# Scan decays of two mixers: differences of cumulative log sums, spread by DMA and clipped on GpSimd, instead of TensorE products with masks

## The reference

```python
def segsum(a):
    cs = jnp.cumsum(a, axis=-1)
    diff = cs[..., :, None] - cs[..., None, :]
    mask = jnp.tril(jnp.ones((l, l), dtype=bool))
    return jnp.where(mask, diff, -jnp.inf)

decay = jnp.exp(segsum(adt))                                  # per chunk and head, 128 x 128
y_diag = jnp.einsum('bcgjls,bcsgjp->bclgjp', cb[:, :, :, None] * decay, xg)
```

## Time and profile before

| | us |
|---|---|
| runs of the kernel, median of 3 | 1102.46 (1102.23 to 1104.29) |
| span of the profiled execution, first to last instruction | 1102.2 |
| TensorE busy | 1065.5 (97%) |
| VectorE busy | 662.8 (60%) |
| ScalarE busy | 442.9 (40%) |
| GpSimd busy | 215.7 (20%) |
| DMA, mean rate over the span | 112 GB/s |

### The profile page before, as it was taken

How to read it: one execution, slowest core, us unless ns; L and a number is a source line. 1 busy time by engine, 2 the same in 40 slices (tenths; PEclk the granted TensorE clock), 3 DMA queues, 4 the chain that set the end, 5 groups by cost and what they waited for, 6 DMA issues and landing times. The chain is left out here.

```text
span 1102.2 us, 14509 instructions
## 1 busy us (share of the span) xinstructions
PE 1065.5 (97%) x5590; PEld 876.1 (79%) x5590; DVE 662.8 (60%) x1139; ACT 442.9 (40%) x826; POOL 215.7 (20%) x161
## 2 busy tenths in 40 slices
PE   9999999999989999999899999999999988989997
PEld 5888888888778877788778788887888866878886
DVE  4246435741056687766736866666595667966635
ACT  4223224332256562231623334348624448225432
POOL 0000000000000052201300100002104754135792
PEclk9999999999989999999999999999999999999999
DMA  8276634322042050232324345435212231203501
GB/s 301 81 271 215 215 102 145 114 80 95 11 136 56 10 197 5 73 134 77 125 77 153 115 153 191 153 115 172 91 63 77 63 111 58 77 20 103 185 1 77
DMA packets 58306, 123.89 MB, mean 112 GB/s; under 512 B 5760, under 2 KB 6016, under 8 KB 58112
## 3 DMA queue, kind: packets, MB, share of 16 engines
q1 hardware_dynamic: 55792, 110.22, 29.9%
q0 software_dynamic: 2304, 12.58, 3.2%
q10 hardware_dynamic: 144, 0.20, 0.0%
HBM read 108.83 MB, written 14.16 MB: 112 GB/s over the span
## 5 line engine op out<-in xcount | busy, mean ns | idle before, releaser
L287 DVE TENSOR_TENSOR w_lo<-raw,w_hi 128x2048 fp32r<-128x2048 f32 x58 | 134.3, 2315 | 207.9 <-ACT w_hi L283 196.9
L283 ACT ACTIVATE w_hi<-raw 128x2048 fp32r<-128x2048 f32 x51 | 97.6, 1913 | 211.4 <-PE projections_ps L131 138.3
L129 PE MATMUL projections_ps<-projections_x_hi,w_hi 128*128 128x512 f32 x208 | 81.1, 390 | 0.4 <-ACTq L506 0.4
L130 PE MATMUL projections_ps<-projections_x_lo,w_hi 128*128 128x512 f32 x208 | 80.9, 389 | 0.0
L131 PE MATMUL projections_ps<-projections_x_hi,w_lo 128*128 128x512 f32 x208 | 80.9, 389 | 0.0
L129 PE MATMUL projections_ps<-w_hi,projections_x_hi 128*128 128x512 f32 x192 | 74.7, 389 | 0.0
L130 PE MATMUL projections_ps<-w_lo,projections_x_hi 128*128 128x512 f32 x192 | 74.7, 389 | 0.0
L131 PE MATMUL projections_ps<-w_hi,projections_x_lo 128*128 128x512 f32 x192 | 74.7, 389 | 0.0
L244 DVE SCALAR_TENSOR_TENSOR resid<-resid,mixer_cw 128x512 f32<-128x512 f32 x96 | 64.9, 745 | 0.0
L2480 POOL TENSOR_TENSOR mixer_es<-masks,mixer_gsel 128x1024 f32<-128x1024 f32 x8 | 17.3, 2165 | 229.5 <-PE mixer_ps L1902 152.2
L129 PE MATMUL output_ps<-w_hi,output_m_hi 128*128 128x512 f32 x128 | 52.9, 413 | 2.5 <-DVE output_m_lo L1267 1.4
(11 more groups left out here) (330 smaller groups left out, 2583.3 us busy)
## 6 DMA issues: line engine op xcount, KB each, us to landing
raw<-in_w_in SPq DMA_DIRECT2D x26, 1024.0 KB, 5.0
raw<-in_gdn_w_in SPq DMA_DIRECT2D x24, 1024.0 KB, 5.0
tok<-in_ada_w POOLq DMA_DIRECT2D x16, 768.0 KB, 6.3
raw<-in_w_out SPq DMA_DIRECT2D x8, 1024.0 KB, 5.0
qkv_kept<-mixer_ring SPq DMA_DIRECT2D x8, 1024.0 KB, 4.2
mixer_st<-qkv_kept SPq DMA_DIRECT2D x32, 256.0 KB, 2.9
raw<-in_gdn_w_out SPq DMA_DIRECT2D x8, 1024.0 KB, 5.1
resid<-in_att_bias SPq DMA_DIRECT2D x16, 256.0 KB, 2.7
```

What stands on the lines that cost most here:

```text
L129: nc.tensor.matmul(out, w_hi, x_hi, start=first, stop=False, skip_group_check=True)
L130: nc.tensor.matmul(out, w_hi, x_lo, start=False, stop=False, skip_group_check=True)
L283: self.nc.scalar.activation(self.hi[s][:], self.raw[s][:], ACT.Copy).then_inc(self.hi_ready, 1)
L287: engine.tensor_tensor(self.lo[s][:], self.raw[s][:], self.hi[s][:], ALU.subtract)\
```

## The change

The cumulative sums of the log decays are now made once per mixer, by two small products: one transposed (heads and chunks on the partitions, `logs_t`), one straight (positions on the partitions, `logs`). `logs_t` is written to device memory. For each step or pair, SP loads its eight rows of 128 values, 4 KB, spread to all 128 partitions, 512 KB in all, into `steps_in` or `steps`. GpSimd subtracts the position's own sum and takes the minimum with 0, one instruction for each head and chunk, in place. ScalarE takes the exponential from SBUF instead of PSUM. The products L1015 and L1902 go, and with them TensorE's waits for steps and exponentials. In the scan, the sums are made at the start of attention; in the mixer, ahead of conv block 4. In the mixer the semaphores of the stages before are cleared by GpSimd.

```diff
@@ attention, TensorE and ScalarE
+            nc.tensor.matmul(ps_o[0:LOGS, 1, 0:P], flat_adt, masks[:, UPPER, :], start=True, stop=True)
+            nc.tensor.matmul(ps_o[:, 1, P:P + LOGS], masks[:, UPPER, :], flat_adt, start=True, stop=True).then_inc(logs_made, 1)
...
+                    nc.scalar.activation(logs_t[0:LOGS, :], ps_o[0:LOGS, 1, 0:P], ACT.Copy).then_inc(logs_out, 1)
@@ scan_and_output, SP
+            def load_logs(s):
+                g = s % G
+                if s >= G:
+                    sp.wait_ge(e_ok, s - 1)
+                sp.dma_start(steps_in[:, g].rearrange("p h l -> p (h l)"), a["logs"][s].partition_broadcast(P))\
+                    .then_inc(logs_in[g], 16)
+
+            sp.wait_ge(logs_kept, 16)
+            for s in range(G):
+                load_logs(s)
             sp.dma_start(resid[:], a["x"].rearrange("(t p) d -> p t d", p=P)).then_inc(rows_in, 16)
...
-            for u in range(2, 6):
+            for u in range(2, 4):
                 load_unit(u)
+            for s in range(G, STEPS - 1):
+                load_logs(s)
+            for u in range(4, 6):
+                load_unit(u)
+            load_logs(STEPS - 1)
@@ TensorE, ahead_of
-                pe.wait_ge(steps_ok, s + 1)
-                if s:
-                    pe.wait_ge(e_ok, s)
-                for n in range(2):
-                    mm = nc.tensor.matmul(ps[:, SEG + n, :], below, steps_in[:, g, 4 * n:4 * n + 4, :].rearrange("p a b -> p (a b)"),
-                                          start=True, stop=True)
-                mm.then_inc(seg_made, 1)
@@ ScalarE
-                act.wait_ge(seg_made, s + 1)
+                act.wait_ge(steps_ok, s + 1)
...
-                nc.scalar.activation(E[:, g], ps_seg, ACT.Exp).then_inc(e_ok, 1)
+                nc.scalar.activation(E[:, g], steps_in[:, g], ACT.Exp).then_inc(e_ok, 1)
@@ GpSimd
-                nc.gpsimd.tensor_tensor(steps_in[:, g], upper.unsqueeze(1).broadcast_to([P, HPG, P]),
-                                        adt[:, c, heads_of(g)].unsqueeze(2).broadcast_to([P, HPG, P]), ALU.mult)\
-                    .then_inc(steps_ok, 1)
+                pool.wait_ge(logs_in[g], 16 * (s // G + 1))
+                for n in range(HPG):
+                    h = g * HPG + n
+                    ins = nc.gpsimd.tensor_scalar(steps_in[:, g, n, :], steps_in[:, g, n, :], logs[:, c, h:h + 1], 0.0,
+                                                  ALU.subtract, ALU.min)
+                ins.then_inc(steps_ok, 1)
@@ second_mixer, SP
+            def load_logs(i, j):
+                if j:
+                    sp.wait_ge(e_ok, at(i, 1, j - 1, 1))
+                elif i:
+                    sp.wait_ge(z_ok, 8 * (HB - 1))
+                else:
+                    sp.wait_ge(logs_kept, 16 * TT)
+                sp.dma_start(flat(steps), a["logs2"][i * HB + j].partition_broadcast(P)).then_inc(logs_in, 16)
...
             stage(0, 2)
+            load_logs(0, 1)
             load(B_CONV + 2)
             sp.wait_ge(kk_made, at(0, 1, 1, 1))
             stage(0, 3)
+            load_logs(0, 2)
             sp.wait_ge(kk_made, at(0, 1, 2, 1))
             stage(0, 0)
+            load_logs(0, 3)
...
             stage(1, 2)
+            load_logs(1, 1)
             sp.wait_ge(kk_made, at(1, 1, 1, 1))
             stage(1, 3)
+            load_logs(1, 2)
             sp.wait_ge(kk_made, at(1, 1, 2, 1))
             stage(1, 0)
+            load_logs(1, 3)
@@ TensorE, build
-                pe.wait_ge(steps_ok, at(i, 1, j, 1))
-                if j:
-                    pe.wait_ge(e_ok, at(i, 1, j - 1, 1))
-                if i and j == HB - 1:
-                    pe.wait_ge(m_lo_ok, 8)
-                for n in range(2):
-                    mm = nc.tensor.matmul(psZ[:, n, :], below, flat(steps[:, 4 * n:4 * n + 4, :]), start=True, stop=True)
-                mm.then_inc(seg_made, 1)
@@ ScalarE, exps
-                act.wait_ge(seg_made, at(i, 1, j, 1))
+                act.wait_ge(steps_ok, at(i, 1, j, 1))
...
-                nc.scalar.activation(E, psZ[:].rearrange("p n (m c) -> p (n m) c", c=P), ACT.Exp).then_inc(e_ok, 1)
+                nc.scalar.activation(E, steps, ACT.Exp).then_inc(e_ok, 1)
@@ GpSimd, log_decay_steps
-                nc.gpsimd.tensor_tensor(steps, upper.unsqueeze(1).broadcast_to([P, 8, P]),
-                                        gs.unsqueeze(2).broadcast_to([P, 8, P]), ALU.mult).then_inc(steps_ok, 1)
+                pool.wait_ge(logs_in, 16 * (at(i, 1, j, 1)))
+                for m in range(2 * TT):
+                    h, c = 2 * (i * HB + j) + m // TT, m % TT
+                    ins = nc.gpsimd.tensor_scalar(steps[:, m, :], steps[:, m, :], logs[:, c, h:h + 1], 0.0,
+                                                  ALU.subtract, ALU.min)
+                ins.then_inc(steps_ok, 1)
```

More of the change, by code:

```diff
@@ L298, in channels @@
             for e in range(4):
+                if s == 0 and e == 3 and before_last:
+                    before_last()
                 for kk in range(HALF):
@@ L665, in _, with attention @@
                     w.tokens(pe, i * 2 + (N_Z + j), (N_Z + j) % 2, ps, x_hi, x_lo, banks_free)
-def attention(nc, a, ahead, mix_in, raw, m_g, resid, masks, qk, vals, tok, bias_in):
+def attention(nc, a, ahead, mix_in, raw, m_g, resid, masks, qk, vals, tok, bias_in, adt, logs, logs_t, logs_kept):
     ctx = Phase(nc, "attention")
@@ L868, in _, with scan_and_output @@
                     exponentials(a_next, TILES[3:])
-def scan_and_output(nc, a, ahead, wba, wba_in, mix_in, split, raw, att_f, m_g, masks, small, resid, row_f, tok, xbc, dt, adt, modc,
-                    g_col, gain):
+def scan_and_output(nc, a, ahead, wba, wba_in, mix_in, split, raw, att_f, m_g, masks, small, resid, row_f, tok, xbc, dt, adt, logs,
+                    logs_kept, modc, g_col, gain):
     w_v = a["w_out"][0].rearrange("(k p) c -> p k c", p=P)
@@ L1433, in second_mixer @@
     NB, HB = 2, 4
+    ended = Phase.take_used()
     ctx = Phase(nc, "mixer2")
@@ L1688, in _ @@
                 if n == 6:
+                    sp.wait_ge(logs_out, 2)
+                    rows_out = a["logs2"].rearrange("r (x c l) -> c (r x) l", c=TT, l=P)
+                    for c in range(TT):
+                        sp.dma_start(rows_out[c], logs_t[V_HEADS * c:V_HEADS * (c + 1), :]).then_inc(logs_kept, 16)
                     sp.wait_ge(spilled[0], 32)
@@ L2253, in _ @@
                         w.round(act, s, b + 1)
+                if b == LOGS_AT - 1:
+                    act.wait_ge(logs_made, 1)
+                    bank = ps[:, 4 * (LOGS_AT % 2) + 3, :]
+                    nc.scalar.activation(logs_t[0:LOGS, :], bank[0:LOGS, 0:P], ACT.Copy).then_inc(logs_out, 1)
+                    nc.scalar.activation(flat(logs[:]), bank[:, P:P + LOGS], ACT.Copy).then_inc(logs_out, 1)
                 act.wait_ge(w.units_used, b * 2 + 4)
```

65 lines of the change are left out of this document (42 added, 23 removed).

## The result

The changed kernel takes 1133.35 us, median of 4 runs (1133.11 to 1136.3), the kernel before 1102.35 us (1101.37 to 1104.29): ratio 1.029, 95% interval 1.0273 to 1.0306. The prediction was 1094.1 us, with 1087 to 1106 as its range. Sign and size are wrong.

A forecast was written before the change was run, and what follows sets the result against it. TensorE, busy 97%, was taken to bound the kernel, except where it waits for others. Scan 10.3, first group +1.3, second group -2.0, small products -1.2 gave 8.4 us less: 1093.8 span, 1094.1 us median, range 1087 to 1106.

The forecast's parts named there:

- TensorE's saving: Removed products in scan and mixer: 1.72 us per step or pair, 27.5 us of TensorE; 10.3 us gained in the scan.
- 10.3 if VectorE can follow: Scan: six steps gain 1.72 us each, provided VectorE's 9.5 us of work fit into steps of 9.7 us.
- The first exponential: even: Scan start: the first exponential has its input at 392.4, against 392.5 before, so no gain or loss.
- weights come a buffer ahead: SP's queue: the next weights stand behind its new wait for the logs, but are loaded early enough; no cost counted.
- GpSimd's price: Eight subtract-and-clip instructions per step or pair take 3.2 us, between 1.9 and 5.4.
- The loop: Mixer, one buffer `steps`: load, GpSimd and exponential follow in turn; first group +1.3 us, second group -2.0 us.
- D: One turn of the mixer's loop, load plus GpSimd plus exponential plus hand-overs: 8.0 us, bounds 6.7 and 13.1.
- the second group: Second group of heads in the mixer: fourth exponential and VectorE's inverse come 2.0 us later, a loss of 2.0 us.
- the sign it set: Second group of heads: TensorE's wait before the inverse's first use grows beyond 4.4 us.
- Small products: Four added products that make the sums, two per mixer, cost about 1.2 us of TensorE, nothing hiding them.
- Port rival: Scan: GpSimd's clipping and skip hold up VectorE, steps take 11.0 us, total 1101.9 us; chance 0.15.
- Long-loop rival: Mixer: the spread load takes 8.7 us, one loop turn 13.1 us, total 1114.4 us; decides from 10.1 us on; chance 0.17.

The follow-up runs named there:

- e13: Kernel before with the change in attention and first scan alone, plus mended instruction orders on ScalarE, GpSimd and VectorE: 1099.76 us, ratio 0.9977.
- e1: Changed kernel with GpSimd making the attention factor `att_f` right after the skip of step 0, ahead of step 2's subtractions: 1119.01 us.
- e8: Kernel before with changed attention and first scan, `att_f` made after step 0's skip, and ScalarE's high parts and weight rounding ahead of the first exponential: 1102.1 us.
- e5: Kernel before with only the unused tile ahead of `ha_hi` grown by 160 words, no instruction changed: 1110.0 us, ratio 1.0062.
- e4: Changed kernel with the unused tile ahead of `ha_hi` at 144 words, putting the activations 256 words from their old place instead of 160: 1130.62 us.
- e14: Kernel before with the changed attention (sum products, copies, transfer), whose results nobody reads: 1100.69 us, ratio 0.999.
- e15: Changed kernel with the mended orders of the scan on all three queues and the mixer's activations 256 words from their old place: 1113.03 us, ratio 1.0091.

## Why the prediction was wrong, step by step

- **TensorE's saving, right.** 1.72 us a step, steps of 9.7 us. But six of them were counted, 10.3 us. In e13, with all three orders mended, the distances from step to step are 9.7, 15.7, 9.7, 12.5, 9.6 and 8.7 us against 10.6, 11.4, 11.4, 11.5, 11.3 and 10.4 before: two of the six are longer, one behind the third exponential, one where VectorE's remainders of the next weights come 2.4 us late (before, they were just in time). Sum of the six: 66.6 -> 65.9, 0.7 us. "10.3 if VectorE can follow" named VectorE's load as the condition. VectorE was busy 15.23 of 19.5 us (435 to 454.5 in the changed kernel, 78%), under the 90% that the text wanted to see, and it was no bound by its load; what failed is when its and GpSimd's results came, and that a stage which gets faster runs into the next limit.
- **"The first exponential: even", failed.** The transfer took 6.1 us from issue to GpSimd's start (382.38 to 388.48), not 3.6, and the subtractions took over 7 us beside VectorE, not 3.2: 13.7 us from issue to the exponential's input, not 6.8. The text then asked only about the exponential, not about what ScalarE had queued behind it; TensorE waited 7.29 us. In e1 that wait was still there (6.6 us) and the stage was 1.0 us shorter than before, so it was paid for by the shorter steps.
- **Order in GpSimd's queue, missing from the sum.** The largest term, 14.6 us. The prediction quoted `att_f`'s row as a price and did not ask where it would stand. The subtractions of steps 2 and 3, which used to run ahead of time out of SBUF alone, now wait for transfers, and everything behind them on GpSimd waits too. The order on SyncE, put at nothing in the text ("weights come a buffer ahead"), is part of it: 6.9 us from the free slot to the issue for step 2, of which GpSimd stood idle 5.86. From e8 on, where ScalarE rounds those weights earlier, it was issued at once (399.43 in e13).
- **GpSimd's price, mis-sized.** 3.2 us, at most 5.4; measured 5.5 alone and 7.6 beside VectorE. The bounds came from a wide two-operand instruction and from tiny ones, and neither is kin to a TENSOR_SCALAR of 128 columns. The Trainium skill, GPSIMD Engine Reference, section Performance versus the Vector engine, gives about 1.8 cycles per element as the best case of a loop; eight of them would be 2.8 us by that, an estimate with the memset's 0.16 us as a start. The trace says twice that, and the trace decides.
- **The loop, right in mechanism, mis-sized by GpSimd's term.** D was 10.5, not 8.0, by GpSimd alone: 3.8 + 5.5 + 1.06 + 0.2 = 10.6. With it the prediction's own line gives -2.0 - 3 x 2.5 = -9.5 for the second group; measured -8.7. For the first: 1.3 - 2.5 = -1.2; measured -3.9, ScalarE's wait holding a bank of z (6.6 us in the waits, where 3.8 was forecast) longer than worked out. By the text's own 4 us per us of D this moves 1094.1 only to about 1104.3, inside its range; the loop by itself does not explain 1133. And the sign it set, a longer wait before the inverse's first use, hardly came: 4.6 us against 4.4. The waiting stands earlier, 4.2 us before the fourth build and 5.5 us before the first `y_pair`, both for what ScalarE and VectorE do only behind the exponentials of 945.56 and 956.20.
- **Placement, not thought of.** 4.0 us in the projections and up to 2 elsewhere, 6 to 7 in all, by e5 (5.9 by the spans, 7.2 by the medians); given back, it was worth 2.7 by the medians of e4.
- **Small products, the sign not borne out.** -1.2 forecast; at the start of attention they seem to have given back more by the clock than they cost, at the edge of what e14 could tell. The projections take 0.7 us more with the placement mended (e4 and e15), which may be theirs.
- **Port rival.** It had the right pair of engines and the wrong victim: VectorE's masking took 1.23 us, and GpSimd's eight went from 5.5 to 7.6. Its one 2.07 fell beside `skip`, a TENSOR_TENSOR, which itself took 2.95 us instead of 1.05, as the 2.50 of the earlier trace rows did beside another. The Trainium skill, GPSIMD Engine Reference, section Key points, says that the two share their SBUF interfaces, and these traces agree that each can hold the other up. Which one loses depends on the pair. In the earlier trace rows GpSimd's TENSOR_TENSOR had begun first and kept its 1.90 us, and VectorE's product ended 1.1 us after it. Beside the TENSOR_SCALARs it is GpSimd that loses: VectorE's masking took 1.23 to 1.24 us in the midst of them in e13.
- **Long-loop rival.** Its condition, D over 10.1, came true through GpSimd's price, which the text put "just on that line" and gave no chance of its own.

The sum with the measured terms: scan stage +16.1, waits of 14.6 for `att_f` and 7.3 behind the first exponential, less what the shorter steps give; mixer loop +8.7 and some +3; placement +6; attention -3.

## What to carry to other kernels

When work moves onto an engine that was idle, write down that engine's whole queue in order and ask of each later instruction, however small, who waits for it. Price an instruction by a row of the same form and size, and if there is none, let the bound be wide enough to change the sign. When tiles are added or removed, look at the distance from one product to the next in a window that has no wait: a stage can be 2% slower with TensorE busy throughout.

## What the runs showed of the hardware that was not expected

- 512-column products in the projections, with `ha_hi` and all tiles behind it 160 words further on in SBUF: 0.232 us from one to the next instead of 0.227, at a full clock; 64, 128 or 256 words further: 0.227.
- GpSimd, TENSOR_SCALAR of 128x128: 0.71 us, 0.58 with one operation, 0.61 with constants; 128x1024 with one operation 2.8 to 3.0 us, while a TENSOR_TENSOR of that size takes 1.9.
- GpSimd's eight TENSOR_SCALARs beside VectorE: 7.0 to 7.6 us instead of 5.5 where VectorE's instructions work on SBUF, and up to 9.3 in one step of e13, with transfers beside them too; 5.55 where they read PSUM.
- Two small products in the gap at the start of attention go with a granted clock of 0.96 to 1.00 in the window 310:320 in all eleven kernels that have them, and 0.76 to 0.87 in the six without.
